# Joining the value and score matmuls of sliding-window attention into one group on TensorE

## The reference

```
h  = rms_norm(x, g_mix) * (1 + sc1) + sh1            # sc, sh, ga: from the vector c
z  = h @ w_in + b_in                                  # width 6400
q, k, v, conv_b, conv_c, conv_x, gate_a, gate_c = split(z)
attn = sliding_window_sink_attention(q, k, v, sinks)  # 16 q heads, 2 kv heads of 64, window 128
conv = conv_b * causal_depthwise_conv(conv_c * conv_x, conv_w)    # 3 taps
x  = x + ga1 * ((sigmoid(gate_a) * attn + sigmoid(gate_c) * conv) @ w_out)
h  = rms_norm(x, g_ffn) * (1 + sc2) + sh2
g, u = split(h @ w_ffn_in)
x  = x + ga2 * ((silu(g) * u) @ w_ffn_out)
return rms_norm(x, g_final)
```

## Time and profile before

| what | value |
|---|---|
| median of 3 runs | 1080.26 us (1079.46 to 1082.6) |
| profiled execution | 1080.09 us, its slowest core's span 1078.5 us |
| spans of the 8 cores | 1069.0 to 1078.5 us |
| PE, DVE, ACT, POOL busy | 90%, 55%, 35%, 19% of the span |
| mean granted TensorE clock, core 0 | 0.971 |
| one chunk in the steady part | 51.2 us |

### The profile page before, as it was taken

How to read it: one execution, slowest core, us unless ns; L and a number is a source line. 1 busy time by engine, 2 the same in 40 slices (tenths; PEclk the granted TensorE clock), 3 DMA queues, 4 the chain that set the end, 5 groups by cost and what they waited for, 6 DMA issues and landing times.

```text
span 1078.5 us, 15320 instructions; the slowest of 8 cores (1069.0 to 1078.5 us)
## 1 busy us (share of the span) xinstructions
PE 967.5 (90%) x5476; PEld 453.7 (42%) x5571; DVE 588.3 (55%) x849; ACT 372.5 (35%) x574; POOL 201.4 (19%) x266
## 2 busy tenths in 40 slices
PE   0569978989999999999898889999999999999993
PEld 0335433434444444444333344444444444444452
DVE  1036785568587877878778642234222243354456
ACT  4287553454445454545233411100111100233232
POOL 2000211212121212122456310000100001213301
PEclk9699998989999999999999999999999999999997
DMA  9960456686821303042802232210522203010112
GB/s 186 220 172 1 64 101 93 87 130 107 267 40 20 47 13 56 6 59 36 131 10 28 51 59 40 40 20 1 88 40 40 40 1 55 14 79 1 79 79 79
DMA packets 43498, 72.25 MB, mean 67 GB/s; under 512 B 19472, under 2 KB 21776, under 8 KB 40352
## 3 DMA queue, kind: packets, MB, share of 16 engines
q0 software_dynamic: 20448, 45.36, 27.1%
q1 hardware_dynamic: 22976, 25.91, 8.0%
HBM read 108.15 MB, written 8.45 MB: 108 GB/s over the span
## 4 chain that ended last, share of the span: by engine, by line
PE 78%; DMA 6%; DVE 5%; issue 4%; ACT 4%; POOL 2%; DVEq 0%; ACTq 0%; POOLq 0%
PE psum L584 29%; PE psum L953 27%; PE psum L966 14%; DMA wadaB<-w_ada_l 5%; PE psum L736 3%; PE psum L900 2%; PE psum L712 2%; POOL acc L892 1%; DMA ws<-w_out_l 1%; PE psum L468 1%; DVE h L917 1%; DVE h L485 1%; DVE xres L984 1%; DVE rs L473 1%; ACT xn L493 1%
## 5 line engine op out<-in xcount | busy, mean ns | idle before, releaser
L584 PE MATMUL psum<-h,ws 128*128 128x512 bf16 (+1 forms) x1696 | 363.1, 365 | 20.4 <-issue 5.2
L953 PE MATMUL psum<-h,fws 128*128 128x512 bf16 x1380 | 307.6, 382 | 10.3 <-DVE xres L906 5.6
L584 PEld LDWEIGHTS psum<-h,ws 128*128 128x128 bf16 x1744 | 161.8, 98 | 193.1 <-issue 41.3
L953 PEld LDWEIGHTS psum<-h,fws 128*128 128x128 bf16 x1408 | 138.3, 98 | 179.6 <-issue 17.4
L961 DVE TENSOR_TENSOR mg<-psum,sg 128x512 bf16<-128x512 f32 x88 | 59.9, 689 | 195.4 <-PE psum L953 195.4
L958 ACT ACTIVATE sg<-psum 128x512 bf16<-128x512 f32 x88 | 52.5, 597 | 318.6 <-PE psum L953 306.0
L966 PE MATMUL psum<-mg,fwo 128*128 128x512 bf16 (+1 forms) x747 | 152.4, 363 | 5.8 <-DVE mg L961 3.3
L761 DVE RECIPROCAL rden<-rden 128x256 f32<-128x256 f32 x64 | 111.9, 1748 | 16.2 <-ACT rden L759 15.7
L973 DVE SCALAR_TENSOR_TENSOR xres<-psum,modc,xres 128x512 f32<-128x512 f32 (+1 forms) x104 | 73.5, 709 | 82.2 <-PE psum L966 80.7
L966 PEld LDWEIGHTS psum<-mg,fwo 128*128 128x128 bf16 x760 | 74.1, 98 | 83.9 <-issue 6.8
L775 POOL TENSOR_TENSOR mg<-nrm,cv 128x256 bf16<-128x256 f32 x64 | 52.0, 816 | 262.6 <-DVE cv L681 170.0
(11 more groups left out here) (84 smaller groups left out, 663.1 us busy)
## 6 DMA issues: line engine op xcount, KB each, us to landing
ws<-w_in_l POOLq DMA_DIRECT2D x50, 256.0 KB, 4.9
fws<-w_fi_l POOLq DMA_DIRECT2D x44, 256.0 KB, 4.7
xres<-xtok SPq DMA_DIRECT2D x8, 1024.0 KB, 11.0
wadaB<-w_ada_l POOLq DMA_DIRECT2D x8, 1024.0 KB, 13.0
xres<-xt SPq DMA_DIRECT2D x8, 1024.0 KB, 18.9
out<-xres SPq DMA_DIRECT2D x12, 512.0 KB, 2.7
fwo<-w_fo_l POOLq DMA_DIRECT2D x22, 256.0 KB, 5.7
wadaA<-w_ada_l POOLq DMA_DIRECT2D x4, 512.0 KB, 19.5
```

The costliest lines, as they stand in the source:

```text
L584: P.op("pe", [lambda e, k=k: e.matmul(bank(b)[:, 0:n], lhsT=WS[s * 1024 + k * 128, s * 1024 + (k + 1) * 128], rhs=hk(k, col, n), start=(k ...
L953: P.op("pe", [lambda e, k=k, w=w, wo=wo, b=b: e.matmul(bank(b), lhsT=w[wo + k * 128, wo + (k + 1) * 128], rhs=hk(k, 128 + tt * 512, 512), ...
```

## The change

The value matmuls of step s-1 (A and B) and the score matmuls of step s become one operation. The program has ten of them in each chunk instead of nine steps: the first has scores only, the last the values of step 8 only. `post` of tile s-2 follows the operation s. The planner's cost of the joined operation is the sum of its parts plus 0.1.

```diff
-        def scores(c, s):
+        def score_part(c, s):
...
-            P.op("pe", fns, reads=ivs, writes=[pv_(4, 2)], cost=0.17 + 0.11 * len(kbs(s)))
+            return fns, ivs, [pv_(4, 2)], 0.1 + 0.11 * len(kbs(s))
+
+        def weights_of(c, s):
...
-        def pv(c, s, o):
+        def pv_part(c, s, o):
...
+            fns, bks = [], []
             if s > 0:
-                P.op("pe", part(2 * s - 1, 6 + (s - 1) % 2, 128, 128, 0, False), reads=ivs(2 * s - 1), writes=[pv_(6 + (s - 1) % 2)], cost=0.25)
-                post(c, s - 1)
+                fns += part(2 * s - 1, 6 + (s - 1) % 2, 128, 128, 0, False)
+                bks.append(pv_(6 + (s - 1) % 2))
             if s < 8:
                 bk = 6 + s % 2
-                P.op("pe", part(2 * s - 1, bk, 0, 128, 128, True) + part(2 * s, bk, 0, 256, 256, False),
-                     reads=ivs(2 * s - 1) + ivs(2 * s), writes=[pv_(bk)], cost=0.6)
+                fns += part(2 * s - 1, bk, 0, 128, 128, True) + part(2 * s, bk, 0, 256, 256, False)
+                bks.append(pv_(bk))
+            ivs = [VS.iv(2 * s * 128, min(2 * s + 2, 17) * 128), ONESB.iv(), PT.iv(o, o + 1024)]
+            return fns, ivs, bks, 0.1 + 0.04 * len(fns)
...
         def attn(c, s):
-            o = scores(c, s)
-            pv(c, s, o)
+
+            fns, ivs, bks, cost = [], [], [], 0.0
+            for part in ([pv_part(c, s - 1, held[s - 1])] if s > 0 else []) + ([score_part(c, s)] if s < 9 else []):
+                fns, ivs, bks, cost = fns + part[0], ivs + part[1], bks + part[2], cost + part[3]
+            P.op("pe", fns, reads=ivs, writes=bks, cost=cost + 0.1)
+            if s < 9:
+                held[s] = weights_of(c, s)
+            if s > 1:
+                post(c, s - 2)
...
-                if i >= first and steps < 9 and (i - first) % 2 == 1:
+                if i >= first and steps < 10 and (i - first) % 2 == 1:
                     attn(c, steps)
                     steps += 1
-            while steps < 9:
+            while steps < 10:
```

More of the change, by code:

```diff
@@ L739, in part @@
                 return out
-            def ivs(kb):
-                return [VS.iv((kb + 1) * 128, (kb + 2) * 128), ONESB.iv(), PT.iv(o, o + 1024)]
+            fns, bks = [], []
             if s > 0:
-                P.op("pe", part(2 * s - 1, 6 + (s - 1) % 2, 128, 128, 0, False), reads=ivs(2 * s - 1), writes=[pv_(6 + (s - 1) % 2)], cost=0.25)
-                post(c, s - 1)
+                fns += part(2 * s - 1, 6 + (s - 1) % 2, 128, 128, 0, False)
+                bks.append(pv_(6 + (s - 1) % 2))
             if s < 8:
                 bk = 6 + s % 2
-                P.op("pe", part(2 * s - 1, bk, 0, 128, 128, True) + part(2 * s, bk, 0, 256, 256, False),
-                     reads=ivs(2 * s - 1) + ivs(2 * s), writes=[pv_(bk)], cost=0.6)
+                fns += part(2 * s - 1, bk, 0, 128, 128, True) + part(2 * s, bk, 0, 256, 256, False)
+                bks.append(pv_(bk))
+            ivs = [VS.iv(2 * s * 128, min(2 * s + 2, 17) * 128), ONESB.iv(), PT.iv(o, o + 1024)]
+            return fns, ivs, bks, 0.1 + 0.04 * len(fns)
         def post(c, i):
@@ L826, in conv_seq @@
             return seq
+        held = {}
         def attn(c, s):
-            o = scores(c, s)
-            pv(c, s, o)
+            fns, ivs, bks, cost = [], [], [], 0.0
[6 more added lines that the diff above has]
+                post(c, s - 2)
         for c in range(8):
```

## The result

The changed kernel takes 1092.35 us in the median, the kernel before 1082.6 us in the same set of runs. The ratio is 1.0097, 95% interval 1.0074 to 1.0120, so the change costs 10.5 us (8.0 to 13.0). The forecast of 1081 us and its range up to 1090 were too low. Ratios are taken over undisturbed runs alone; where disturbed runs shift a median, the text goes by the ratio.

A forecast was written before the change was run, and what follows sets the result against it. PE's list of work and its waits were taken to set the end. From 1080.09 us, -4.4 for boundaries, +2.4 for waits and +2.6 at the last chunk's end gave 1080.7, forecast as 1081; range 1074 to 1090, own range 1078 to 1083.

The forecast's parts named there:

- Step 1, boundaries: Chunk loop on PE: tiling-mode boundaries fall from 264 to 224, each 0.11 us, so -4.4 us.
- Step 2, the wait of the joined operation: Chunk loop: A, B and scores wait together for post's bank; loop stays hidden, +2.4 us, bounds 0 and +8.
- a rival: Steady chunks: the one-step loop through banks 6 and 7 takes over, 1087 us at a 7.0 us step; chance 0.33.
- with 2.5 us in hand: Steady chunk: the loop needs 47.9 us and PE 50.4 us, so the loop is hidden by this margin.
- The step of the loop: Mid-chunk distance between joined operations: 5.6 to 7.5 us, taken as 6.3 us.
- the closing piece: Chunk's end, operation 8 to operation 0 of the next: exp, a group in progress and scores, about 2.6 us.
- the point of decision: Steady chunk: the loop sets the chunk's time from a step of 6.7 us on.
- The term for the waits: Waits from lagging attention, such as q groups held up by late scores: 0.3 us a chunk over eight chunks, +2.4 us.
- Step 3, the end of the last chunk: Last chunk's end: last scores not before 520.78 us, two w_out groups lose their place; +2.6 us, bounds 0 and +5.2.
- PE idle ahead of value matmuls, released by L762: Sign of the loop winning: such idle time on PE exceeds 1 us a chunk.
- a chunk over 51.5 us: Sign of the loop winning, read from the length of a steady chunk.
- The sign for my forecast: Middle of a steady chunk: joined operations 5.6 to 6.7 us apart, listed among the signs of being right.

The follow-up runs named there:

- early_sandwich: Changed kernel plus ScalarE's early copy of the numerator out of PSUM, scores placed between A and B in joined operations; ratio 0.9989 to the kernel before.
- early_after: Changed kernel, but ScalarE copies the numerator out of its PSUM bank, so the bank is free earlier; 1077.69 us, ratio 0.9974 to the kernel before.
- copy_hold: Changed kernel with the numerator copied on ScalarE, but the multiply still reads PSUM, so the bank stays held; 1092.08 us, ratio 1.0084 to the kernel before.
- three_banks: Changed kernel without copy, value tiles in three PSUM banks (3, 6, 7) and full groups in three instead of four; ratio 1.0013 to the kernel before.
- post_first: Changed kernel with post written ahead of exp and mask in the program; 1101 us, ratio 1.0172 to the kernel before.
- last_split: Changed kernel, but the last chunk alone keeps scores, A and B separate, with the earlier costs and order; ratio 1.0083 to the kernel before.

## Why the prediction was wrong

**Step 1, boundaries: right.** Forecast 224, counted 220. The price of 0.11 from the earlier trace rows is 0.08 in early_sandwich's period, 0.12 with the waits taken off. So joining did save 44 x 0.08 to 0.12, 3.5 to 5.3 us of PE time, forecast 4.4.

**Step 2, the wait of the joined operation: this step failed.** The mechanism was described, as a loop through banks 6 and 7, and a rival gave it 0.33. But the forecast had the loop hidden, "with 2.5 us in hand", and put 0.3 us a chunk on waits. Measured is 1.8 us more of waiting in chunk 6 (2.0 against 0.2), which after the boundaries saved leaves the chunk 1.0 us longer, where the forecast had it 0.5 us shorter.

The step of the loop was sized well, 6.3 forecast and 6.44 measured in chunk 6. What was mis-sized is the rest of the chunk's round. From the first scores to operation 2 it takes 8.5 us (437.13 to 445.66), forecast 7.5; from operation 8 to the next first scores 5.1 us (484.28 to 489.36), forecast 2.6. I had taken the closing piece as if only exp and a group lay in it. And the point of decision, a step of 6.7 us, was worked out from these too small pieces: with 13.6 for them it would have been 6.1, below the step that I forecast. One caution: the steps and the end pieces of any chunk add up to its period, whatever bounds it, so their sum of 52.2 us doesn't prove the loop. The waits do.

The lag also builds up, which the sum for a single chunk leaves out. In chunk 3 the steps are 6.87 us in the mean and PE waits for no other engine, but operation 8 starts only 2.5 us ahead of the next first scores, where early_after has 13.1 us. In chunks 4, 5 and 6 the waits are then 1.0, 2.1 and 2.0 us.

The term for the waits was +2.4 us. On core 0 the last chunk starts 8.3 us late although 39 boundaries fewer lie before it, so the waits there are about 12 us more. 4.0 of the 8.3 are there at chunk 3 already. I had counted the loop for the five steady chunks alone, in the rival too, whence 1087 instead of 1092. Why the first three chunks lose as much was not tried by itself; between 137 and 211 us PE waits 3.8 us for L765 and 3.8 us for the mask, so the loop is in the open there too. copy_hold against early_after and three_banks show that it is the bank; post_first shows that the mask shares the loop.

One row was misread: in the window of 174 to 225 us PE doesn't wait for w_ada. Its waits there are 2.1 us for exp, 1.3 for L667, 0.9 for L762 and 0.8 for the mask, so part of today's time in the early chunks is attention's own chain already. The one wait for w_ada nearby, 1.6 us, ends at 164 us.

**Step 3, the end of the last chunk.** The place was right: the last scores come behind 520.78, at 537.69. The forecast was +2.6. From the first scores of the last chunk to the end core 0 loses 0.7 us, the median of the eight cores 4.2. last_split gives back 1.5 us by the ratios, with overlapping intervals. It doesn't give back the lag that the chunk inherits. The place where that lag shows I had not seen at all: not idle time at 512 to 523, but the wait of 9.35 us for the second norm at 572. It is 4.9 us in last_split, and early_after has no such wait. Its length isn't the loss, though: last_split's first feed-forward group is 6.0 us earlier than the changed kernel's (575.6 us), and its core 0 ends only 0.3 us earlier.

**The marks.** Of the signs listed, "PE idle ahead of value matmuls, released by L762" came (L765 here, 1.11 us in the chunk shown), as did a chunk over 51.5 us. The sign for my forecast, operations 5.6 to 6.7 us apart, came too, and so was no mark to tell the two apart. The rule of the Trainium skill on tiling modes (TensorEngine Tiling (Array Packing), Key Properties: changing the mode drains the array) agrees with early_sandwich, which adds only such changes: the period grows by 0.54 us. That it is the draining that takes this time is not shown.

**The clock.** In the joined steady chunk it stays at 1.00. The 0.91 at 545 to 600 us comes with the one long wait. It is no part of the 1%: the mean granted clock of core 0 is 0.971 in both kernels, and from 600 to 700 us it is 0.98 before and 1.00 in the changed one.

## What to carry to other kernels

Joining operations also joins their waits: each part then waits for the latest input of all, and a double-buffered resource that served two steps in flight serves one. A lag that one round leaves is paid in the next. Before joining, write down the whole round, with the pieces at its ends, and hold it against the engine that bounds the kernel; a margin of 5% in such a sum is no margin. If the round is too long, free the contended buffer first (here a 0.4 us copy, worth 6 us without joining), and then ask whether joining still gains anything; here no gain was measured.

## What the runs showed of the hardware

A wait of PE of 9.35 us ends at the lower clock: in the changed kernel's windows, ahead of, in and behind that wait, the granted clock is

```profile
560.00:572.00 12.00, 8.90 (x37) 3.32 (x36) 10.32 (x6) 6.23 (x10) 10.28 (x9) 1.00 0.00 1
572.00:581.60 9.60, 0.25 (x2) 0.02 (x1) 9.60 (x15) 0.00 (x0) 1.21 (x1) 0.78 0.00 0
581.60:586.00 4.40, 4.39 (x11) 1.62 (x12) 4.40 (x6) 3.27 (x5) 2.74 (x2) 0.50 0.00 0
```

In the last window it is 0.50, 1.2 GHz, and PE gets through 11 matmuls of 512 columns in 4.4 us where 20 fit at 0.216 us each. From 586 to 588 us the granted clock is 0.60, from 588 us on 1.00. So the wait costs 2 to 3 us more than its own length.

Shorter waits differ. Those of 1.11 us and less in the steady chunk leave the clock at 1.00, and so does the wait of 2.42 us ahead of 537.13 (window 516.16 to 540.46); the wait of 2.05 us in the kernel before is followed by 0.56.
